# Attention and linear-attention trunk on one core: three pieces of weight preparation moved on VectorE, one projection piece moved on TensorE

## What is computed

```python
xn = rms_norm(h, norm1_g)
gq, gk, gv, gr, glr, dq, dk, dv = split(xn @ w_in)
o_gla = gla_mixer(gq, gk, gv, gr, glr, ...)      # linear attention, 4 heads, chunk scan with a carried state
o_diff = diff_attention(dq, dk, dv, ...)         # 4 heads, two softmaxes each, p1 - lam * p2, then @ v, then a norm
h = h + concat([o_gla, o_diff]) @ w_out
h = h + hier_moe(rms_norm(h, norm2_g), ...)      # top-1 of 4 groups, top-2 of 8 experts
```

## Time and profile before

| what | value |
|---|---|
| median of 3 runs | 1206.89 us (1206.07 to 1207.35) |
| the profiled execution, its own time | 1205.52 us |
| its span | 1203.8 us |
| PE busy | 1138.5 us, 95% of the span |
| DVE busy | 887.1 us, 74% |
| ACT busy | 693.5 us, 58% |
| POOL busy | 263.4 us, 22% |
| mean granted clock of PE | 0.984 |

### The profile page before, as it was taken

The page is one execution under the profiler, slowest core; times in us unless marked ns, Lnnn a source line. Parts: engine busy times, 40 slices in busy tenths (PEclk is TensorE's granted clock), DMA queues, the critical chain, the costliest instruction groups (busy, mean ns, idle before and its releaser), DMA issues. The chain is left out here.

```text
span 1203.8 us, 17123 instructions
## 1 busy us (share of the span) xinstructions
PE 1138.5 (95%) x5875; PEld 862.7 (72%) x5876; DVE 887.1 (74%) x1312; ACT 693.5 (58%) x915; POOL 263.4 (22%) x326
## 2 busy tenths in 40 slices
PE   6999999899999889999599999999999999999993
PEld 5868887666777678888467777777777777777772
DVE  4424424656576788887688999999999989999882
ACT  5424202454455643343367777777777777777771
POOL 2212103412121221223442121221221221212100
PEclk9999999999999999999799999999999999999997
DMA  8130210200200444343699999999999999999941
GB/s 318 41 106 1 105 58 13 71 35 27 97 27 9 150 143 144 136 171 140 228 391 387 375 394 379 374 399 376 377 391 371 383 383 371 391 380 367 399 148 27
DMA packets 67426, 273.34 MB, mean 227 GB/s; under 512 B 13156, under 2 KB 19880, under 8 KB 42664
## 3 DMA queue, kind: packets, MB, share of 16 engines
q1 hardware_dynamic: 56744, 245.32, 52.7%
q0 software_dynamic: 7168, 20.98, 7.6%
q10 hardware_dynamic: 3456, 6.29, 1.4%
HBM read 248.44 MB, written 28.32 MB: 230 GB/s over the span
## 5 line engine op out<-in xcount | busy, mean ns | idle before, releaser
L1953 DVE TENSOR_TENSOR main_w_low<-w_raw,main_w_high 128x2048 fp32r<-128x2048 f32 x190 | 434.5, 2287 | 50.7 <-ACT main_w_high L1949 50.6
L1949 ACT CAST main_w_high<-w_raw 128x2048 fp32r<-128x2048 f32 x190 | 362.3, 1909 | 74.9 <-PE main_score L1969 52.6
L1877 POOL DMA_INDIRECT main_xg<-xn_dram,main_token x32 | 75.9, 2371 | 372.7 <-DVE main_token L1857 365.8
L1967 PE MATMUL main_pt<-main_w_high,main_xT_high 128*96 128x512 f32 x256 | 103.4, 404 | 1.2 <-DVE main_xT_low L2110 1.2
L1967 PE MATMUL main_score<-main_w_high,main_hT_high 128*96 128x512 f32 x256 | 102.5, 400 | 1.2 <-DVE main_hT_low L2122 1.2
L1969 PE MATMUL main_pt<-main_w_high,main_xT_low 128*96 128x512 f32 x256 | 101.9, 398 | 0.0
L1969 PE MATMUL main_po<-main_w_high,main_xT_low 128*96 128x512 f32 x256 | 101.2, 395 | 0.0
L1968 PE MATMUL main_pt<-main_w_low,main_xT_high 128*96 128x512 f32 x256 | 101.1, 395 | 0.0
L1967 PE MATMUL main_po<-main_w_high,main_xT_high 128*96 128x512 f32 x256 | 100.7, 393 | 0.0
L1969 PE MATMUL main_score<-main_w_high,main_hT_low 128*96 128x512 f32 x256 | 100.7, 393 | 0.0
L1968 PE MATMUL main_po<-main_w_low,main_xT_high 128*96 128x512 f32 x256 | 100.6, 393 | 0.0
(11 more groups left out here) (309 smaller groups left out, 2311.6 us busy)
## 6 DMA issues: line engine op xcount, KB each, us to landing
w_raw<-in_moe_w SPq DMA_DIRECT2D x192, 1024.0 KB, 18.3
slot_raw<-in_w_in SPq DMA_DIRECT2D x12, 1024.0 KB, 7.4
main_x<-in_x SPq DMA_DIRECT2D x8, 512.0 KB, 11.1
slot_raw<-in_w_out SPq DMA_DIRECT2D x4, 1024.0 KB, 6.8
main_hx<-in_x SPq DMA_DIRECT2D x8, 512.0 KB, 3.9
out<-main_hx SPq DMA_DIRECT2D x8, 512.0 KB, 2.9
xn_dram<-main_xn SPq DMA_DIRECT2D x8, 512.0 KB, 2.9
gr_dram<-main_stage ACTq DMA_DIRECT2D x8, 256.0 KB, 2.0
```

The source lines that it names most:

```text
L1877: nc.gpsimd.indirect_dma_start(xg[u][:], None, s["xn2_dram"], bass.IndirectOffsetOnAxis(token[u][:, 0:1], 0), bounds_check=bound["x"], oob ...
L1949: nc.scalar.copy(wh[slot(c, e)][:], raw[u][c // 2][:, c % 2, :]).then_inc(w_high, 1)
L1953: nc.vector.tensor_tensor(wl[slot(c, e)][:], raw[u][c // 2][:, c % 2, :], wh[slot(c, e)][:].bitcast(F32), ALU.subtract).then_inc(w_low, 1)
L1967: nc.tensor.matmul(out, x_hi, w_hi, start=start, stop=False)
```

## The change

The low part of a half of chunks 4, 5 and 6 is made by DVE one step later than ACT makes the high part: still behind the maxima (and the query sum) of the step, but of step m + 1. The low part of (7, 1) goes behind the norm of item 30, the 31st, which is step 33's. One piece of the last `gv` unit goes from step 30 to step 31. ACT's order changes only in that the spill of that unit, which follows its end, is now in step 31.

```diff
-    sizes = [6] * (N - 2 * HD) + [4, 4, 4, 3, 3, 3, 3]
+    sizes = [6] * (N - 2 * HD) + [4, 4, 4, 3, 3, 3, 2, 1]
...
-            if m in split_at:
-                weight_low(*split_at[m])
+            if m - 1 in split_at:
+                weight_low(*split_at[m - 1])
             if m >= N:
                 norm(m - 3)
+            if m == N + 1:
+                weight_low(7, 1)
             if m == N:
                 turned_low("d", 0)
                 exponents(0)
                 dve_then(dve, nc.vector.memset(sc[:], 0.0))
                 nc.vector.memset(state[:], 0.0).then_inc(state_ready, 1)
                 scale_qk(0)
-                weight_low(7, 1)
```

## The result

| what | before | changed |
|---|---|---|
| median | 1207.12 us (1205.26 to 1208.05, 8 runs) | 1210.86 us (1209.29 to 1214.73, 8 runs) |
| ratio to before, 95% interval | | 1.0034 [1.0025, 1.0042] |
| the profiled execution, its span | 1205.52, 1203.8 us | 1211.58, 1209.8 us |
| PE busy | 1138.5 us | 1145.4 us |
| mean granted clock of PE | 0.984 | 0.977 |

A forecast was written before the change was run, and what follows sets the result against it. PE, busy nine tenths or more in most slices, was taken as the bound, so only its idle stretches could be won. -5.9 (low parts) + 2.9 (tail) = -3.0 us, giving 1203.9 us; range 1200.2 to 1206.9, to 1206.8 with the second rival.

The forecast's parts named there:

- the price of the piece: End of the attention: the later spill delays SP's tiles and `inner(0)` by 3.3 us; tail 2.9 us lost net.
- The spill's landing: Last spill's DMA, behind two 1 MB loads: lands at 416.9, bounds 415.3 and 417.6.
- The tile's landing: SP's first tile load, behind the spill: lands 2.6 us after its start, at 419.5, 3.3 us late.
- Taking the piece out of step 30: PE ahead of the scores of item 31: little gained, since item 30's exponentials end at 405.64; 0.1 us.
- ACT's 1.0 us: Spill ahead of the square of item 29 makes item 30's values 1.0 us late; swallowed by the 3.3 us.
- The rule on the spill's landing: DMA queues taking turns let the spill in between SP's loads: landing near 415.3, tail loses 1.3 us; chance 0.20.
- The low parts: Six low parts in chunks 4 to 6, one step later: DVE's waits cover them; 5.9 us gained, bounds 4.0 and 7.3.
- the forecast's first point: First sign of being right, on DVE: no low part waits for `slot_high`.
- (4, 1): Its low part, behind the query sum: 0.3 us gained, with a new wait of about 1.4 us before item 8's scores.
- the second rival: Norm between DVE's two maxima waits for POOL's root: 3.0 us of the gains go, 1206.9 us; chance 0.22.
- (7, 1): Its low part behind the norm of item 30: 0.3 us gained of PE's 0.99 us wait before item 31's values.
- The slower rival: Low parts not covered, DVE sets the pace behind them: 7.0 us lost, 1210.9 us; chance 0.08.

The follow-up runs named there:

- e4: The changed kernel with the old table of pieces, so without the moved piece: 1203.06 us.
- e2: The kernel before with only the piece moved from step 30 to step 31: 1216.55 us.
- e8: The changed kernel with 20 more matmuls, whose result nobody reads, in PE's wait ahead of `inner(0)`: 1208.02 us.
- e5: The changed kernel, with SP loading the first linear-attention chunk's tiles before the two halves of chunk 7: 1209.8 us.
- e10: e9 with the last spill behind the square of item 29 on ACT: 1206.37 us.
- e11: e7 with the piece moved, half (7, 0) loaded behind the first chunk's tiles, and the last spill behind ACT's square of item 29: 1206.52 us.
- e9: The changed kernel, with only half (7, 1) loaded ahead of SP's wait for the spill and (7, 0) behind the first chunk's tiles: 1207.61 us.
- e3: The kernel before with only the low part of (7, 1) moved behind the norm of item 30: 1206.94 us.
- e7: e4 with the low part of (4, 1) ahead of the query sum of step 6: 1200.13 us.
- e12: The same kernel as e7, run again on another chip: 1200.02 us.
- e1: The kernel before with only the low parts of chunks 4, 5 and 6 one step later: 1204.06 us.

## Why the prediction was wrong

**The step that failed is the price of the piece**, "Tail: 3.3 - 0.3 - 0.1 = 2.9 us lost (bounds 0.6 and 4.0)". Its mechanism was right at the links of this chain: ACT's spill one step later, SP's 7.7 us again, the exponents waiting for `b_tile`, PE idle ahead of `inner(0)`. Its size was 6.6 us at `outer(0)`, and 7.8 (e4) to 9.4 us (e2) in the time. Counted from the scores of item 31, the links read:

| link | before | changed | difference | forecast |
|---|---|---|---|---|
| SP's first tile load | 7.01 | 11.99 | +4.98 | +4.0 |
| `b_tile`, from load to exponents | 2.6 (landing) | 3.63 | +1.0 | 0 |
| exponents (L1449) | 10.38 | 15.62 | +5.24 | +3.3 |
| `inner(0)` (L757) | 15.93 | 21.41 | +5.48 | +3.3 |
| `outer(0)` (L772) | 20.53 | 27.16 | +6.63 | +2.9 |
| later, on PE | | | +2.7 more, of which 2.25 also in e4 without the piece | 0 |

- *The spill's landing* was taken at 416.9, 4.0 us late. It was 5.0 late, at the late bound and a little past it. The landings say why: the second load landed at 413.1 before and 413.5 in the changed kernel, the spill at 412.8 and 414.0, with the loads both times.
- *The tile's landing* was taken at the median of 2.6 us, and took 3.63, in a queue that had just delivered 2 MB. I had priced it from a median over many landings in which the queue was less busy.
- *The clock* had no term at all. I had written "so it is idle", and priced 3 us of idle time at 3 us. Behind the idle time the next two rows of PE took 1.37 us longer (2.08 and 1.11 against 1.16 and 0.66), 1.15 of which reached `outer(0)`. Filling the wait (e8) gained 2.8 us in the median, of which its trace ties 0.98 to the wait.
- *Taking the piece out of step 30* gained 0.07 us up to the scores of item 31 in e2's trace (forecast 0.1).
- *ACT's 1.0 us* showed at another place than forecast. The spill also stands ahead of the copy of the transposes, so PE's second transposes wait 1.62 us in place of 0.73. In the changed kernel the tile swallowed it, as I had said. It was not free, though: all seven traces with the moved piece show a half clock somewhere between 410 and 436, behind this wait (e5, e8, e10, e11) or in and behind a later one (the changed kernel, e2, e5, e9). None of the seven traces without it does. The sum had nothing for that.

**The rule on the spill's landing.** The wait of SP is 7.7 us again in the changed kernel. From the spill's start to SP's release it is 2.1 us without loads (e5), and 2.1 us behind one load (e9). The changed kernel's two loads, and below them its spill:

```profile
L217 SPq DMA_DIRECT2D slot_raw<-in_w_out x2: 367/438/508, 405.5 to 405.9; - x2
DMA to landing us min/median/max: 4.9/6.2/7.6
...
L1002 ACTq DMA_DIRECT2D gv_dram<-main_stage x1: 327/327/327, 409.5 to 409.5; - x1
DMA to landing us min/median/max: 4.5/4.5/4.5
```

Read as I did, the rule of the Trainium skill, "DMA: Bandwidth & Descriptors", section "Queues, rings and completion order", that each DMA engine takes turns between its queues, would have let the spill in behind two loads as well. The landings don't come out so: SP was released 4.6 us after the spill's start, when the loads had landed. They don't show when the spill's own packets moved, so they speak against what I made of the rule, and not against the turns themselves. Why two loads hold it and one does not was not tried further. In e9 only 0.9 us of the one load were left when the spill was started, so a load that runs beside the spill for its whole length was never tried alone.

**The low parts** (six by a step; the title counts their three chunks) were forecast at 5.9 us and gave 4.5 in the attention. No wait of a low part is left, and their cover was there: the forecast's first point was right. (4, 1) gained nothing, where 0.3 was forecast: its waits in steps 6 to 8 are 0.65, 0.37, 0.97 and 0.71 us, and before they were 1.11, 0.63 and 0.62. The last of these, ahead of the scores of item 8 (242.06), is missing from the earlier trace rows; there the forecast wanted a wait of over 1 us, and 0.71 came. Of the 1.4 us missing, 1.1 stand around 243, where the clock was low: e4 runs the same instructions up to there with the clock at 1.00 and gains 5.6 us. So the forecast of this part was nearly right for an execution without the low stretch. How much of it is chance is open: of the eight traces with this order seven show it, e4's alone does not, and none of the other six does, neither before, e2 and e3, whose low parts stand in their old place, nor e7, e11 and e12, which have (4, 1) ahead of the sum. The root of POOL named by the second rival was never what PE waited for behind step 8.

**(7, 1)**: 0.3 forecast, 0.24 measured (e3).

**The rivals.** The slower rival named 1210.9 us, and the time was 1210.86, by coincidence. Its mechanism, low parts without cover, did not occur, since there is no bracket in the steps behind them, and e1, which has them alone, is faster. A slower outcome through the tail was what I should have listed: 6.6 us lost there, against 4.5 gained, needed only the late bound of the spill, a slower tile and the clock. The range ended at 1206.8, since my bounds of the tail ended at 4.0.

**What stays open.** Why the half clock shows at 420 to 427 in e9, and between 410 and 416 in e5, e8, e10 and e11, although their waits just ahead are under 2 us each, why short stretches of it come around 242 and 565 in some versions or executions, and with these what the piece costs once the spill is no longer held. That wasn't tried.

## What to carry to other kernels

A piece of work that ends a producer carries everything behind it: when it moves by a step, follow every DMA that its end releases, in the order in which the queue will start them, and take the late bound for a small DMA that is started behind large ones on which a whole engine waits. Give idle time of PE a range above its length, since the clock can fall behind it: here 5.28 us of it made the next two rows 1.37 us longer. And a preparation step on a vector engine is best put not only behind its input, but into a place where that engine waits for something else anyway (e7: 0.6% faster than before, with the six low parts and (7, 1), which alone changed nothing that can be told in e3).

## What the runs showed of the hardware

- Twenty unread matmuls in a wait of 5.28 us made the kernel 2.8 us faster. From 417 to 427 the clock was 1.00, while without them it was 0.50 from 423 to 427, and `inner(0)` took 2.08 us and not 1.16.
- The clock was low again 140 us later, in 570 to 575, in the kernel with the idle stretch, and not in e8, though PE's work in between is the same. e1 and e4, which have no such idle stretch, also show a low stretch near 561 to 566, so the link is not shown.
- Waits of PE of 1.62 to 1.64 us were followed by a half clock of some microseconds in e5, e8, e10 and e11 (values of item 30: 3.36 to 3.65 us and not 2.02). In the changed kernel and in e9, with the same wait of 1.62 us, these values took 2.02 us.
- A DMA of 256 KB took 2.1 us from its start to the release of its waiter when no load was under way (e5), 2.1 us behind one load of 1 MB that had 0.9 us left (e9), and behind two 6.7 us (before) and 4.6 (the changed kernel). With two loads it landed within 0.5 us of the second one's landing.
